# Gate and signal loads behind the signal's scatter, another order of banks and copies in a long convolution, and four moved pieces of work

## The reference

```python
def bidir_long_conv(z, h_fwd, h_bwd, bias):
    k = jnp.concatenate([h_fwd, jnp.zeros_like(h_fwd[:1]), h_bwd[1:][::-1]], axis=0)
    kf, zf = jnp.fft.rfft(k, n=2 * L, axis=0), jnp.fft.rfft(z, n=2 * L, axis=1)
    return jnp.fft.irfft(zf * kf, n=2 * L, axis=1)[:, :L] + z * bias

def hyena_mixer(h, ...):
    u = short_conv(h @ w_in + b_in, conv_w, conv_b)
    x1, x2, v = jnp.split(u, 3, axis=-1)
    filt = hyena_filters(...)
    z = v
    for n, gate in enumerate((x1, x2)):
        z = gate * bidir_long_conv(z, filt[:, n, 0], filt[:, n, 1], fbias[n])
    return z @ w_out + b_out
```

## Time and profile before

| | |
|---|---|
| median of 3 runs | 3555.58 us |
| the profiled execution | 3557.13 us, span 3555.5 us |
| mean granted TensorE clock | 0.966 |
| TensorE matmuls busy | 3246.7 us, 91% |
| VectorE busy | 2162.5 us, 61% |
| ScalarE busy | 1286.1 us, 36% |
| POOL busy | 312.9 us, 9% |
| chain that ended last | PE 74%, DVE 13%, DMA 6%, ACT 3%, issue 3% |

### The profile page before, as it was taken

One profiled execution on the slowest core, in us unless ns is written; L12 is line 12 of the kernel. 1 busy time (PEld: TensorE's weight loads), 2 busy tenths in 40 slices (PEclk: granted clock), 3 DMA queues, 4 the chain that ended last, 5 costly groups with the idle time before them and its releaser, 6 DMA issues.

```text
span 3555.5 us, 49957 instructions
## 1 busy us (share of the span) xinstructions
PE 3246.7 (91%) x19458; PEld 2554.6 (72%) x19458; DVE 2162.5 (61%) x3209; ACT 1286.1 (36%) x2121; POOL 312.9 (9%) x508
## 2 busy tenths in 40 slices
PE   7999888988698999998999889999999979999897
PEld 4888545655476888887788667777778758887685
DVE  6998654444466555454768556555556576655676
ACT  3112333333344333332445433333334253333344
POOL 0111234444200000000000200000000000000000
PEclk8999999999899999999999999999999989999999
DMA  7555656567702322224434310000002133333532
GB/s 293 203 200 201 212 150 168 138 180 180 231 25 67 114 92 86 84 83 186 151 96 164 122 53 10 8 7 7 7 25 78 48 113 104 101 107 118 213 99 88
DMA packets 183696, 410.14 MB, mean 115 GB/s; under 512 B 33263, under 2 KB 60207, under 8 KB 180791
## 3 DMA queue, kind: packets, MB, share of 16 engines
q1 hardware_dynamic: 131288, 270.56, 22.9%
q0 software_dynamic: 51936, 131.27, 12.6%
q10 hardware_dynamic: 288, 5.77, 0.4%
HBM read 262.38 MB, written 81.00 MB: 97 GB/s over the span
## 4 chain that ended last, share of the span: by engine, by line
PE 74%; DVE 13%; DMA 6%; ACT 3%; issue 3%; POOL 1%; SPq 1%; DVEq 0%; ACTq 0%; POOLq 0%
PE ps L655 19%; PE ps L657 19%; PE ps L656 19%; PE ps L2518 3%; PE ps L2452 2%; PE ps L2491 2%; PE ps L2470 2%; PE ps L2351 2%; PE ps L725 1%; DVE mx L2907 1%; DMA t2z<-s 1%; PE ps L2553 1%; DMA traw<-hidden_scratch 1%; DMA t2k<-s 1%; DMA wraw<-in_w_in 1%
## 5 line engine op out<-in xcount | busy, mean ns | idle before, releaser
L655 PE MATMUL ps<-HB,gsp 128*128 128x512 f32 x1232 | 487.9, 396 | 38.7 <-DVE HB L831 21.9
L656 PE MATMUL ps<-HB,gsp 128*128 128x512 f32 x1232 | 484.2, 393 | 0.0
L657 PE MATMUL ps<-HB,gsp 128*128 128x512 f32 x1232 | 483.2, 392 | 0.0
L1109 DVE TENSOR_TENSOR gsp<-graw,gsp 128x512 fp32r<-128x512 f32 x330 | 226.4, 690 | 262.3 <-ACT gsp L1088 261.5
L1088 ACT ACTIVATE gsp<-graw 128x512 fp32r<-128x512 f32 x330 | 206.5, 628 | 325.6 <-PE ps L657 266.5
L655 PEld LDWEIGHTS ps<-HB,gsp 128*128 128x128 f32 x1232 | 234.0, 190 | 92.4 <-issue 21.4
L655 PE MATMUL ps<-tsp,wdh 128*128 128x512 f32 x616 | 243.6, 395 | 35.6 <-DVE tsp L1366 35.6
L657 PEld LDWEIGHTS ps<-HB,gsp 128*128 128x128 f32 x1232 | 233.7, 190 | 49.7
L656 PEld LDWEIGHTS ps<-HB,gsp 128*128 128x128 f32 x1232 | 234.1, 190 | 46.4 <-issue 1.0
L656 PE MATMUL ps<-tsp,wdh 128*128 128x512 f32 x616 | 241.4, 392 | 0.0
L657 PE MATMUL ps<-tsp,wdh 128*128 128x512 f32 x616 | 241.2, 392 | 0.0
(11 more groups left out here) (279 smaller groups left out, 7446.0 us busy)
## 6 DMA issues: line engine op xcount, KB each, us to landing
graw<-in_w_gu SPq DMA_DIRECT2D x176, 256.0 KB, 2.7
mring<-in_mod_w POOLq DMA_DIRECT2D x78, 512.0 KB, 4.5
hidden_scratch<-R SPq DMA_DIRECT2D x154, 256.0 KB, 2.4
traw<-hidden_scratch SPq DMA_DIRECT2D x154, 256.0 KB, 2.6
t2k<-s POOLq DMA_DIRECT2D x80, 256.0 KB, 5.6
t2z<-s POOLq DMA_DIRECT2D x160, 128.0 KB, 4.6
t2w<-w POOLq DMA_DIRECT2D x160, 128.0 KB, 3.2
wd<-in_w_dx SPq DMA_DIRECT2D x6, 2816.0 KB, 14.3
```

What stands on the lines that cost most here:

```text
L655: pe.matmul(o, wh, xh, start=start, stop=False, skip_group_check=onto)
L656: pe.matmul(o, wh, xl, start=False, stop=False, skip_group_check=onto)
L657: return pe.matmul(o, wl, xh, start=False, stop=stop, skip_group_check=onto)
L1109: dve.tensor_tensor(gsp[U % 3][:, 1, :], graw[:, q, W_SLOT[i], :], gsp[U % 3][:, 0, :].bitcast(F32), ALU.subtract).then_inc(w.lo, 1)
```

## The change

Gate and signal: the load of the gate of order 1 moves from B(it,0) to Z(it,1) for it < 4, and there both it and the load of the next signal wait until the scatters of Z(it,1) have landed. The load of mi moves ahead of the last store of u. Two of the eight x tiles are loaded at M(4,0); the other five of the first seven no longer wait for the w1 scatters, and go in another order. S(it,0) uses banks 6 and 7 for even units, 4 and 5 for odd ones, and TensorE waits for the signal's eviction ahead of unit 1 and not of unit 0; ScalarE copies unit 0 ahead of the evictions still open. `last_mods` goes ahead of VectorE's copies in S(0,0). `modulations` move to K(2,3), K(3,3) and K(4,3).

```diff
-        SETS_C, SETS_D, SETS_S = ((4, 2), (0, 6)), ((6, 0), (4, 2)), (4, 6)
+        SETS_C, SETS_D, SETS_S = ((4, 2), (0, 6)), ((6, 0), (4, 2)), ((6, 4), (4, 6))
@@ sync
             store_u(22, 0)
+            sp.wait_ge(p_in.full, 24 * 6)
+            sp.dma_start(mi[:], a["k_mi"][:, 0]).then_inc(s_ci, 16)
             store_u(23, 1)
             sp.wait_ge(s_us[0], 12 * 32)
             sp.wait_ge(s_us[1], 12 * 32)
-            sp.wait_ge(p_in.full, 24 * 6)
-            sp.dma_start(mi[:], a["k_mi"][:, 0]).then_inc(s_ci, 16)
             sp.dma_start(mib[:], a["k_mi"][:, 1]).then_inc(s_ci, 16)
...
                     if o == 1 and it + 1 < NIT:
                         sp.wait_ge(s_af, A_END["Z", it, 1])
+                        sent(sp, B_END["Z", it, 1])
+                        sp.wait_ge(s_ae, A_END["B", it, 0])
+                        sp.dma_start(share(gbuf, it), u_share(it, 1)).then_inc(s_gl, 16)
                         sp.dma_start(share(zbuf, it + 1), u_share(it + 1, 2)).then_inc(s_zl, 16)
...
                     sp.dma_start(share(gbuf, it), u_share(it, 0)).then_inc(s_gl, 16)
+                    if it == NCH:
+                        sp.wait_ge(s_ae, K_DONE[2 * NCH - 1])
+                        sp.wait_ge(s_bf, KB_AT[-1] + 1)
+                        for k in range(2):
+                            sp.dma_start(R[:, k, :], a["x_t"][:, k, :]).then_inc(s_x2, 16)
                 elif kind == "B" and o == 0:
-                    if it < NCH:
-                        sp.wait_ge(s_ae, A_END["B", it, 0])
-                        sp.dma_start(share(gbuf, it), u_share(it, 1)).then_inc(s_gl, 16)
-                    else:
+                    if it == NCH:
...
             sp.wait_ge(s_pr, N_Z)
-            sp.wait_ge(s_w1a, 32 * (N_Z // 8))
-            sp.wait_ge(s_w1o, 32 * 7 * (N_Z // 8))
-            for k in MIX_FIRST[0][:KD - 1]:
+            for k in (3, 2, 4, 5, 6):
                 sp.dma_start(R[:, k, :], a["x_t"][:, k, :]).then_inc(s_x2, 16)
@@ scalar
+                elif kind == "S":
+                    act.wait_ge(s_pr, 8 * (2 * it + o))
+                    for u in (0, 2):
+                        act.wait_ge(s_kf, n["k"] + u + 1)
+                        act.activation(kk[...], pair(SETS_S[o][0])..., ACT.Copy).then_inc(s_ke, 1)
+                        for b in range(taken, n["B"]):
+                            sent_out(b)
+                        taken = n["B"]
@@ tensor
                     sent(pe, B_END["K", it, 3])
-                    pe.wait_ge(s_be, n["B"] - 1)
                     for u in range(4):
+                        if u == 1 - o:
+                            pe.wait_ge(s_be, n["B"] - 1)
@@ vector
-            MODULATED = {("S", 1, 0): (0, 0, 3), ("S", 1, 1): (1, 1, 0), ("S", 2, 0): (2, 1, 3)}
+            MODULATED = {(2, 3): (0, 0, 3), (3, 3): (1, 1, 0), (4, 3): (2, 1, 3)}
...
+                    if (it, o) in MODULATED:
+                        modulations(*MODULATED[it, o])
                 elif kind == "S":
+                    if it == 0 and o == 0:
+                        last_mods(LAST_MODS[4:])
                     dve.wait_ge(s_pr, 8 * (2 * it + o))
                     for u in (1, 3):
...
-                    if it == 0 and o == 0:
-                        last_mods(LAST_MODS[4:])
-                    if (kind, it, o) in MODULATED:
-                        modulations(*MODULATED[kind, it, o])
```

More of the change, by code:

```diff
@@ L2152, in _ @@
                     done = quarter
+                elif kind == "S":
+                    act.wait_ge(s_pr, 8 * (2 * it + o))
+                    for u in (0, 2):
+                        act.wait_ge(s_kf, n["k"] + u + 1)
+                        act.activation(kk[:, 1024 * u:1024 * u + 1024].rearrange("p (a r c) -> p r a c", a=2, r=2),
+                                       pair(SETS_S[o][0]).rearrange("p r (a c) -> p r a c", a=2), ACT.Copy).then_inc(s_ke, 1)
+                        for b in range(taken, n["B"]):
+                            sent_out(b)
+                        taken = n["B"]
                 else:
@@ L2164, in _ @@
                         taken = n["B"] + u
[L2165 to L2171, removed]
+                if kind == "M":
                     tail = it == NCH and o == 1
@@ L2422, in _ @@
                                 e = 2 * u + h + 8 * c
-                                mm = pe.matmul(ps[rows64(c), SETS_S[u % 2] + r, CW * h:CW * (h + 1)],
+                                mm = pe.matmul(ps[rows64(c), SETS_S[o][u % 2] + r, CW * h:CW * (h + 1)],
                                                st[rows64(r), const_at(it, e), 0:64],
@@ L2794, in _ @@
                         dve.tensor_copy(kk[:, 1024 * u:1024 * u + 1024].rearrange("p (a r c) -> p r a c", a=2, r=2),
-                                        pair(SETS_S[1]).rearrange("p r (a c) -> p r a c", a=2)).then_inc(s_kd, 1)
-                    if it == 0 and o == 0:
-                        last_mods(LAST_MODS[4:])
-                    if (kind, it, o) in MODULATED:
-                        modulations(*MODULATED[kind, it, o])
+                                        pair(SETS_S[o][1]).rearrange("p r (a c) -> p r a c", a=2)).then_inc(s_kd, 1)
                 elif kind == "Z":
```

## The result

| | before | after |
|---|---|---|
| median | 3556.68 us (3554.17 to 3558.34, 4 runs) | 3529.07 us (3522.02 to 3534.63, 4 runs) |
| profiled execution, span | 3557.13, 3555.5 | 3522.02, 3520.4 |
| granted clock | 0.966 | 0.967 |
| TensorE, VectorE, ScalarE, POOL busy | 3246.7, 2162.5, 1286.1, 312.9 | 3253.3, 2163.8, 1285.4, 312.3 |

The ratio is 0.9922 (0.9903 to 0.9941): 28 us faster, where 51 were forecast. The sign is right, but the time lies above the range, which ended at 3524. The profiled execution happened to be the fastest of the four.

The account below looks back on a forecast made before the run. TensorE's stalls and low clock were taken as the bound, chiefly 27.4 us waiting for scatters ahead of M(it,1). Terms 14.7, 2, 3.5, 7.5, 8, 7.7 and 7.6 summed to 51.0, giving 3504 us, range 3488 to 3524.

Parts of the forecast that it names:

- F: x loads behind the convolution: 3.2 us from two tiles moved to M(4,0), 4.4 from dropping the w1 waits; gain 7.6.
- A: Ahead of M(it,1): gate and signal loads behind the scatter cut TensorE's start to 3.9 us after POOL's end; gain 14.7.
- F's wait "at 5 to 6": Sign of being right: TensorE's wait behind the convolution, 13.24 us before, would be 5 to 6 us.
- Rival 1: Ahead of M(it,1): the tail belongs to the scatters themselves, A and A' give nothing, time 3521 us; chance 0.18.
- A': Low clock behind the four stalls ahead of M(it,1): some 8 us lost, most of it staying; gain 2 us.
- rival 2: All stalls shrink so far that the clock stays up: 62 us off, time 3494; chance 0.14.
- B: Wait of 8.19 us ahead of the first spectrum: mi loaded earlier, gain 3.5 us.
- C: Wait of 7.14 us before the first product: last modulations moved ahead of S(0,0)'s copies, gain 6.5 us plus 1 for clock.
- D: S(it,0): other banks and copy order remove most of the waits of 1.24 and 1.18 us; gain 8 us together.
- E: Modulations moved from S into K(it,3), where VectorE waits anyway: S(2,0) and S(1,1) shorter by 4.2 and 3.5; gain 7.7 us.
- Rivals 3 and 4: Signal late each iteration, slower, 3563 us at a 36 us landing, chance 0.03; waits only change names, 3548 or above, 0.05.

Follow-up runs that it names:

- e11: e3 with only the two waits on the w1 scatters left out, so seven x loads go out beside the last t2w scatters: 3529.17 us, ratio 0.9920.
- e1: The changed kernel run again without an edit: 3530.05 us, ratio 0.9909 to the kernel before.
- e2: The changed kernel with the two w1 waits put back ahead of the five x loads, two tiles still at M(4,0): 3519.10 us, ratio 0.9890.
- e5: e3 with one more wait, SP waiting for the scatters of Z(0,0) before loading the first gate: 3521.78 us, ratio 0.9905.
- e7: The kernel before with only the banks and copies of S(it,0) in another order: 3548.37 us, ratio 0.9976.
- e4: The kernel before with only the gate and signal loads moved behind the scatter: 3549.84 us, ratio 0.9972.
- e12: e5 with the gate and signal loads as in the kernel before: 3527.49 us, ratio 0.9918.
- e10: The kernel before with only mi loaded earlier: 3554.41 us, ratio 0.9992.
- e3: The changed kernel with all x loads as before, seven behind the convolution and behind the w1 waits: 3521.28 us, ratio 0.9902.
- e8: The kernel before with only the three sets of modulations moved from S to K: 3547.30 us, ratio 0.9970.
- e6: The kernel before with only the last modulations ahead of VectorE's copies in S(0,0): 3551.40 us, ratio 0.9980.

## Why the prediction was right and wrong

**F is the step that failed:** "The waits on the w1 scatters fall away ...: 4.4 after its own latency. Between, SP still waits for gbuf at 951.3 ..., so no hole opens." The 3.2 for the early tiles was right as bytes (3.0). The 4.4 had the wrong sign: 2.7 to 5.8 lost in the traces, 8 to 11 by the medians, some 7 by the ratios. I priced the wait by what SP could do earlier and did not ask what those transfers run beside. A's whole argument is that loads on SP stretch POOL's scatters; the same rows applied to t2w give the loss. The hole followed, since the copy of gbuf waits for B(4,1). I took its 951.3 for a fixed time, and it is an event. SP, before:

```profile
951.34 1.36 SPq L1956 DMA_DIRECT2D mix_raw<-gbuf  x1
```

What a run without the waits loses beyond the 3 to 6 us of the traces stays open. The profiled executions of after and e11 were the fastest of theirs. That of e1 was the slowest of its five, 13.9 us longer than e2's: 5.4 of it lies behind M(4,1), where the waits act, but 6.7 lies between K and B(4,0), where the two programs are the same.

F's wait "at 5 to 6" was to show it right; it came to 3.75 with the term wrong. A wait that shrinks proves a gain only if the instruction behind it also starts earlier.

**A was right in mechanism, and too large.** Rival 1 is refuted: most of the tail belonged to the loads, as the two groups of waits show. POOL ended its trains at 501.57, 598.77, 696.04 and 791.74, TensorE started 4.31, 3.98, 4.37 and 5.49 later, where I took 3.9 for each. POOL in order of time, the train of Z(1,1), of the changed kernel:

```profile
589.36 9.41 POOL L2025 DMA_DIRECT2D t2z<-s  x16 [4.91 <-ACT s L2131]
```

The rest of the miss is the one profile I worked from: its 27.4 is the highest of six kernels with the same loads, whose mean is 24.6, and its 8.12 ahead of M(1,1) is 4.38 to 5.33 in the others. I took 8.12 as a constant. The gain in waits is 9.5, not 14.7. Behind POOL's end 4 to 5.5 us remain. (The Trainium skill, "DMA: Bandwidth & Descriptors", anatomy of one SWDGE DMA, would put the start some 1.7 behind that end, by the same estimate as in the prediction. No train of the fourteen profiles came near it: the smallest value ahead of M(it,1) is 3.60, in e5, and ahead of M(0,0) 2.88, in e7.)

A' came, and at about 4 rather than 2. The four stretches from M(it,1) to M(it+1,0), which begin behind the waits, sum to 166.4 us before and 162.2 in e4, and to 154.4 in e12 and 150.4 in e5. In the changed kernel the first 16 matmuls take 1.98, 1.69, 1.09 and 1.99, so at least two of the four stages still began at the low clock; so rival 2, with the clock up throughout, did not come. (The terms named for it sum to 61, not 62.) In the traces A and A' are then worth about 13.5, and by the time of e4 6 to 14, both under 16.7.

**B, C and D** agree with the forecast within their uncertainty, at 2.8, 7.1 and 8.5; for B the 8.19 ahead of the first spectrum became 4.53 in e10. VectorE ended its eight reductions before its first copy was wanted, as C's cover asked. VectorE in order of time, of the changed kernel:

```profile
435.59 0.17 DVE L2655 TENSOR_TENSOR modv<-macc,modb 128x12 f32<-128x12 f32 x1
436.88 1.22 DVE L2805 COPY kk<-ps 128x1024 f32<-128x1024 f32 x1 [1.13 <-PE ps L2430]
```

What C's step left out was a trigger: it listed what the reductions delay, not who waits for their end. That took 2.0 of B and C in the changed kernel's profile (12.96 less 10.97) and 3.7 in e3's.

**E** measured 10.7 against 7.7, within its uncertainty. Its two measured stretches were right, against the changed kernel's busy time by stretch, S(2,0) to M(2,0) and S(1,1):

```profile
628.30:640.80 12.50, 11.95 (x149) 10.04 (x141) 4.52 (x5) 3.89 (x4) 8.09 (x14) 1.00 0.67 181
562.45:585.38 22.93, 20.73 (x192) 11.66 (x192) 10.64 (x15) 8.74 (x13) 5.92 (x11) 1.00 0.37 92
```

In e8's trace the moved work is worth 4.3 from M(1,1) to M(2,0), 3.5 from M(1,0) to the wait ahead of M(1,1), and 0.5 in S(1,0) (13.19 against 13.65 from its start to M(1,0)), so "S(1,0) hid them almost wholly" holds: 8.2 in all. The waits ahead of M(it,1), which E does not touch, happened to be 4.3 shorter in that profile.

**Rivals 3 and 4** did not occur: the signal's load took longer, 12.5 us in the second iteration against 9.0, but the 21 us were enough and no transpose waits for it in the changed kernel; M(it+1,0) does not wait.

The account, by the ratios: 51.0 less 14.7 for F (7.6 gained became 7.1 lost, the changed kernel against e3) and less 8.5 for A to E (43.4 became 34.9) is 28. Of the 8.5, 4.3 is what the parts gave alone less than forecast, above all A, and 4.2 is what they gave less in company. Two causes of the latter are seen in traces, the early gate load and the 2 to 3 us that D and E share; how far they make it up the times cannot tell, at about 4 us for each part.

## What to carry to other kernels

A wait ahead of a load is also a shield for the transfers that run meanwhile: before taking it away, look which scatters the load will run beside, and who waits for them. When work moves, list what its end releases as well as what it delays. And a stall read from one profile is one draw; where a term rests on the largest of several like stalls, take it nearer to the others.

## What the runs showed of the hardware

A short wait can cost more behind itself than in itself. The 64 matmuls of B (64 columns each) took 7.3 us, at a granted clock of 1.00 (2.4 GHz) in before and e3, where the wait ahead of them was none or up to 0.57 us. They took 12.86, 13.89 and 13.85 us (after, e11, e1), at clocks of 0.54 and 0.50 (1.2 GHz nearly throughout), behind waits of 2.32, 3.67 and 3.63, and 11.54 and 11.59 (e2, e1) behind 0.84 and 0.86; and 7.33 once (after) behind 0.86. So at 0.84 to 0.86 the same wait gave both. A wait within the stage did the same: the last 32 matmuls of B(1,1) took 5.8 to 7.1 us behind 0.66 to 0.67 (before, e4, e6, e10), and 3.79 behind 0.73 (e7). What decides between the two is not shown.

Loads on SP's queue stretch POOL's scatters: the t2w scatters of 128 KB landed in 2.1 us alone (before, e3), in 7.0 beside x and z in the changed kernel and in 4.4 in e1; the first t2z train in 3.5 before and 5.7 beside the gate load in e6 (medians).
